# Column sums of shift and scale with 128 stationary columns in one product instead of four products of 32

## What is computed

```
c_act = silu(c)                                   # 1024 values
for i in range(2):
    shift, scale, gate = split(c_act @ mod_w[i] + mod_b[i], 3)     # mod_w[i]: 1024 x 3072
    h = rms_norm(x, norm_g[i]) * (1 + scale) + shift
    y = retention(h, ...) if i == 0 else forgetting_attention(h, ...)
    x = x + gate * y
```

## Time and profile before

| | |
|---|---|
| median of three runs | 694.55 us (694.49 to 694.74) |
| the profiled execution | 694.77 us, its span 693.0 us |
| PE busy | 679.8 us, 98% of the span |
| DVE, ACT busy | 502.2 us (72%), 380.4 us (55%) |
| products and loads of PE | 4590, 4591 records |
| bytes moved | 138.81 MB, 200 GB/s on average |

### The profile page before, as it was taken

The page is one execution under the profiler, slowest core; times in us unless marked ns, Lnnn a source line. Parts: engine busy times, 40 slices in busy tenths (PEclk is TensorE's granted clock), DMA queues, the critical chain, the costliest instruction groups (busy, mean ns, idle before and its releaser), DMA issues.

```text
span 693.0 us, 11560 instructions
## 1 busy us (share of the span) xinstructions
PE 679.8 (98%) x4590; PEld 554.2 (80%) x4591; DVE 502.2 (72%) x803; ACT 380.4 (55%) x561; POOL 16.3 (2%) x35
## 2 busy tenths in 40 slices
PE   8899999999999999999999999999999999999996
PEld 4679997777878888878788877778888888888885
DVE  6888988787986779766768889777665555565445
ACT  5457434565555665654655765845574444444444
POOL 4010000000000000000000000000000000000000
PEclk9999999999999999999999999999999999999999
DMA  9999785667896176833455654434656666655511
GB/s 295 368 377 391 272 265 174 201 223 230 303 339 213 51 245 225 274 128 106 135 157 158 190 164 137 139 122 120 212 156 212 182 190 178 197 185 189 186 61 61
DMA packets 74405, 138.81 MB, mean 200 GB/s; under 512 B 5732, under 2 KB 18400, under 8 KB 74352
## 3 DMA queue, kind: packets, MB, share of 16 engines
q1 hardware_dynamic: 72816, 134.92, 60.1%
q10 hardware_dynamic: 736, 1.81, 0.7%
q0 software_dynamic: 800, 1.35, 0.6%
HBM read 137.01 MB, written 1.05 MB: 199 GB/s over the span
## 4 chain that ended last, share of the span: by engine, by line
PE 90%; DVE 3%; SPq 2%; DMA 1%; ACT 1%; issue 1%; DVEq 0%; ACTq 0%
PE G L392 23%; PE G L394 22%; PE G L393 22%; PE T L433 5%; PE G L412 2%; PE G L413 2%; PE G L414 2%; PE T L791 2%; DMA arena<-in_mod_w_dram 1%; PE T L779 1%; DVE wlo L1119 1%; SPq L2547 1%; PE G L529 1%; PE G L531 1%; PE G L530 1%
## 5 line engine op out<-in xcount | busy, mean ns | idle before, releaser
L1119 DVE TENSOR_TENSOR wlo<-raw,whi 128x1024 fp32r<-128x1024 f32 x202 | 245.6, 1222 | 111.3 <-ACT whi L1927 110.9
L1927 ACT ACTIVATE whi<-raw 128x1024 fp32r<-128x1024 f32 x202 | 211.9, 1060 | 133.4 <-PE G L394 89.5
L392 PE MATMUL G<-whi,ahi 128*128 128x512 f32 x694 | 280.4, 404 | 0.2 <-DVE wlo L1119 0.2
L394 PE MATMUL G<-whi,alo 128*128 128x512 f32 x694 | 271.1, 391 | 0.0
L393 PE MATMUL G<-wlo,ahi 128*128 128x512 f32 x694 | 270.4, 390 | 0.0
L392 PEld LDWEIGHTS G<-whi,ahi 128*128 128x128 f32 x694 | 130.3, 188 | 29.3 <-issue 1.8
L394 PEld LDWEIGHTS G<-whi,alo 128*128 128x128 f32 x694 | 130.3, 188 | 28.4
L393 PEld LDWEIGHTS G<-wlo,ahi 128*128 128x128 f32 x694 | 130.6, 188 | 25.3 <-issue 1.0
L1929 ACT ACTIVATE arena<-T,st 128x128 f32<-128x128 f32 (+2 forms) x56 | 21.8, 476 | 30.0 <-DVE st L1520 30.0
L1927 ACT ACTIVATE ahi<-T 128x512 fp32r<-128x512 f32 x25 | 14.9, 597 | 39.6 <-PE T L433 39.6
L1929 ACT ACT_TABLE_LOAD x27 | 34.6, 1283 | 3.3 <-issue 1.8
(11 more groups left out here) (254 smaller groups left out, 628.8 us busy)
## 6 DMA issues: line engine op xcount, KB each, us to landing
raw<-in_ret_w_in_dram SPq DMA_DIRECT2D x48, 512.0 KB, 6.2
raw<-in_w_gate_up_dram SPq DMA_DIRECT2D x40, 512.0 KB, 4.0
raw<-in_mod_w_dram SPq DMA_DIRECT2D x32, 512.0 KB, 4.7
raw<-in_fox_w_in_dram SPq DMA_DIRECT2D x32, 512.0 KB, 4.6
raw<-in_w_in_dram SPq DMA_DIRECT2D x28, 512.0 KB, 3.7
raw<-in_w_down_dram SPq DMA_DIRECT2D x22, 512.0 KB, 3.5
arena<-in_mod_w_dram SPq DMA_DIRECT2D x16, 512.0 KB, 9.6
raw<-in_ret_w_out_dram SPq DMA_DIRECT2D x16, 512.0 KB, 5.1
```

The costliest lines, as they stand in the source:

```text
L392: e.matmul(o, ah, wh, start=first and k == 0, stop=False)
L394: done = e.matmul(o, al, wh, start=False, stop=last and k == 1)
L1119: e.tensor_tensor(o, a, b, op).then_inc(sig[name], 1)
L1927: d = e.activation(o, a, f, scale=scale)
```

## The change

The diff has four parts. In `own_rows` and `other_rows` the loop over four ranges of 32 columns goes, and one product has 128 stationary columns. POOL waits for the fifth count of `macc` (DVE's sum of the last group) instead of the 12th of `mod0`. The forget gates' high and low parts lie in turns of 16 columns (`narrow`), so that one product of 32 stationary columns gives both the high-by-high and the low-by-high part, in 32 partitions; high by low stays a product of 16. `zT` has 32 rows, and `turn_forget` replaces the transposes by products with a constant matrix that adds row r and row r + 16 while it turns them.

```
-        zT = PTf[0:16, 0, 0:S]
+        zT = PTf[0:32, 0, 0:S]
+        narrow = ahi[:, 29, :].rearrange("p (k t n) -> p k t n", t=2, n=16)
...
                 for r in range(r0, 8):
-                    for c in range(0, P, 32):
-                        e.matmul(o[c:c + 32, :], mod_tile(g)[:, a, r, i * P + c:i * P + c + 32], cact[:, r:r + 1].to_broadcast([P, 32]), start=r == r0, stop=False)
+                    e.matmul(o, mod_tile(g)[:, a, r, i * P:i * P + P], cact[:, r:r + 1].to_broadcast([P, 32]), start=r == r0, stop=False)
...
-                for c in range(0, P, 32):
-                    d = e.matmul(sums_at(SUMMED[g][i], a)[c:c + 32, :], macc[:, g % 2, a, i * P + c:i * P + c + 32], ones[:, 0:32], start=False, stop=True)
-                return d
+                return e.matmul(sums_at(SUMMED[g][i], a), macc[:, g % 2, a, i * P:i * P + P], ones[:, 0:32], start=False, stop=True)
...
             def turn_forget():
                 on_.wait_ge(sig["forget"], 1)
+                on_.wait_ge(sig["head2_in"], 32)
                 t = bank("forget_t", sig["forget"], 2)
                 for m in range(2):
-                    d = e.transpose(t[:, 16 * m:16 * m + 16], zT[:, m * P:(m + 1) * P], idf[0:16, 0:16])
+                    d = e.matmul(t[:, 16 * m:16 * m + 16], zT[:, m * P:(m + 1) * P], head[0:32, C_SEL:C_SEL + 16], start=True, stop=True)
...
-                e.matmul(t[0:16, 0:S], wh, ahi[:, k, :], start=k == 0, stop=False)
-                e.matmul(t[0:16, 0:S], wl, ahi[:, k, :], start=False, stop=False)
-                d = e.matmul(t[0:16, 0:S], wh, alo[:, k, :], start=False, stop=k == 7)
+                e.matmul(t[0:32, 0:S], ahi[:, 29, 32 * k:32 * k + 32], ahi[:, k, :], start=k == 0, stop=False)
+                d = e.matmul(t[0:16, 0:S], narrow[:, k, 0, :], alo[:, k, :], start=False, stop=k == 7)
...
-                    tt(ahi[:, 29, P:2 * P], raw_tile(n), ahi[:, 29, 0:P].bitcast(F32), ALU.subtract, "used")
+                    tt(narrow[:, :, 1, :], raw_tile(n).rearrange("p (k n) -> p k n", n=16), narrow[:, :, 0, :].bitcast(F32), ALU.subtract, "used")
...
-                    copy(zT, T[bank_of["forget"]][0:16, 0:S], "forget")
+                    copy(zT, T[bank_of["forget"]][0:32, 0:S], "forget")
...
-                        act(ahi[:, 29, 0:P], raw_tile(n), ACT.Copy, "narrow_hi")
+                        act(narrow[:, :, 0, :], raw_tile(n).rearrange("p (k n) -> p k n", n=16), ACT.Copy, "narrow_hi")
...
-            on_.wait_ge(sig["mod0"], 12)
+            on_.wait_ge(sig["macc"], 5)
             e.dma_start(posi, pos_in.partition_broadcast(P).rearrange("p a n -> p (a n)")).then_inc(sig["small_in"], 16)
```

More of the change, by code:

```diff
@@ L725, in _ @@
             t = bank("forget", sig["forget"], 1)
-            nhi, nlo = ahi[:, 29, 0:P], ahi[:, 29, P:2 * P]
             for k in range(8):
@@ L729, in _ @@
                 on_.wait_ge(*ready[k, 1])
-                wh, wl = nhi[:, k * 16:(k + 1) * 16], nlo[:, k * 16:(k + 1) * 16]
-                e.matmul(t[0:16, 0:S], wh, ahi[:, k, :], start=k == 0, stop=False)
-                e.matmul(t[0:16, 0:S], wl, ahi[:, k, :], start=False, stop=False)
-                d = e.matmul(t[0:16, 0:S], wh, alo[:, k, :], start=False, stop=k == 7)
+                e.matmul(t[0:32, 0:S], ahi[:, 29, 32 * k:32 * k + 32], ahi[:, k, :], start=k == 0, stop=False)
+                d = e.matmul(t[0:16, 0:S], narrow[:, k, 0, :], alo[:, k, :], start=False, stop=k == 7)
             d.then_inc(sig["forget_pe"], 1)
```

## The result

The changed kernel takes 700.69 us (699.74 to 702.30), the kernel before 694.74 us in the same comparison: the ratio is 1.0088, with a 95% interval of 1.0076 to 1.0100. One of the five executions of the kernel before took 977.55 us, the others 694.49 to 694.88; the ratio leaves it out. The change makes the kernel slower, and by more than the 0.2% that can be told from none. The forecast was 699.4, 1.3 us too little, with a range of 697.7 to 701.0. The profiled execution is the quickest of the five: 699.74 us, its span 697.9 us, 4.9 us longer than before. Its mean granted clock is 0.999. The other executions, 700.4 to 702.3 us, have 0.991 to 0.997; what stands behind that comes with the experiments.

The account below looks back on a forecast made before the run. PE, busy 98% of the span, was taken as the bound, with the sums on the path in each stage. Stages +5.55 and forget gates -0.7 us on 694.55 gave 699.4 us, range 697.7 to 701.0.

Parts of the forecast that it names:

- The price of a 128-column record: PE's sums: each record of 128 stationary fp32 columns takes 110 ns, against 42 ns for four of 32.
- The rival of 42 ns: PE's sums: a 128-column record costs only 42 ns, giving a faster kernel, 693.6 us; chance 0.05.
- The stages: Groups 0 to 4 before the last `rows_unit`: longer sums delay it by 2.65 + 1.4 + 1.5 = +5.55 us.
- PE's wait for `macc`: In front of PE's sums: the wait gets shorter in group 2 and is gone in group 0.
- Forget gates: PE's forget products: 8 of 24 go, -0.91 us, turning costs +0.2; net -0.7 us.
- The moved transfers: DVE's first sum into `acc`: rows of `mod_b` land up to 6.3 us later; cost taken as 0.
- the bound of 1: Upper limit of +1 us for DVE standing at its first sum into `acc` for the moved transfers.
- The sum: Whole kernel: +5.55 - 0.7 = +4.85 us, giving 699.4 us.
- the clock: Behind the sums: PE's clock falls to 1.2 GHz, 2.7 us more once or twice, 702 to 705 us; chance 0.04.
- the late rows of `mod_b`: DVE stands 1 us or more for these rows, and PE with it: 700.4 us; chance 0.06.

Follow-up runs that it names:

- experiment 5: Kernel before with the sums as two products of 64 stationary columns instead of four of 32: 695.87 us, ratio 1.0021.
- experiment 6: Changed kernel with 2 moving columns instead of 32 in the 128-column sums: 703.65 us, ratio 1.0123.
- experiment 3: Kernel before with only POOL's small transfers moved, waiting for `macc` 5 instead of `mod0` 12: 695.90 us, ratio 1.0017.
- experiment 4: Changed kernel with the 32-column sums back, joined forget products and moved transfers kept: 695.61 us, ratio 1.0012.
- experiment 1: Kernel before with only the 128-column sums in `own_rows` and `other_rows`: 702.18 us, ratio 1.0108.
- experiment 10: Changed kernel with POOL's small transfers waiting for `mod0` 12 again: 700.67 us, ratio 1.0086.
- experiment 7: Kernel before with 128-column products in `own_rows` only, `other_rows` keeping its four of 32: 703.21 us, ratio 1.0117.
- experiment 9: Changed kernel with bf16 filler products where PE waits, before the first sums and in group 2: 699.86 us, ratio 1.0075.
- experiment 2: Kernel before with only the joined forget products: 694.07 us, ratio 0.9993.
- experiment 11: Kernel before with joined forget products and, in groups 2 to 4, all own records before the first of DVE's sums: 693.71 us, ratio 0.9987.
- experiment 8: Kernel before with joined forget products and four blocks instead of six for DVE in group 2: 700.32 us median, one execution 694.27.
- experiment 12: Kernel before with 64-column sums and four blocks instead of six for DVE in group 2: 695.90 us, ratio 1.0015.

## Why the prediction was right, and where it fell short

**The price of a 128-column record.** Forecast 110 ns, measured 108 in the changed kernel and 111 with two moving columns. Experiments 5 and 6 show that it is the stationary width of one range. The rival of 42 ns, and with it a faster kernel by wider sums, is out.

**The stages.** Group 2's sums end at 29.87 (29.48 + 0.39), forecast 29.85; `macc` is there at 27.45, forecast 27.5, and ACT's `x0_high` at 19.70, forecast 19.65. The first `rows_unit` behind it is 2.67 us late, forecast 2.65. Group 3 adds 1.24 (forecast 1.4) and group 4 1.47 (forecast 1.5), and the last `rows_unit` starts at 56.10, 5.4 us late, forecast 5.55. That PE's wait for `macc` would get shorter in group 2 was wrong: 0.96 us against 1.02, since DVE and PE moved alike. In group 0 it is gone, as forecast.

**Forget gates.** Net 0.6 of forecast 0.7 us: 16 products of 0.114 us in place of 24 as forecast, the turning 0.1 us dearer than thought.

**The moved transfers.** The place was right, DVE's first sum into `acc`, and so was the cost that I took, none, but only for the changed kernel, and there by luck: DVE comes there at 59.14 instead of 54.22 and finds the rows landed, 1.8 to 2.0 us after their issue and not up to 6.3. My reason for the 0 was another one, that PE uses the low parts behind that sum only 3 to 5 us later; in experiments 3 and 4, where DVE does stand, PE waits for such a low part (0.4 and 0.9 us). Taken alone the edit costs 1.2 us and in experiment 4 about 1.5, above the bound of 1 that I had given, since DVE stood 2.3 and 3.5 us. I had priced the edit behind the delay that another part of the change makes.

**The sum, and the term that it lacks.** 4.85 us were forecast and 4.97 measured between the two profiled executions. The medians are 6 us apart. What I left out of the sum, with a chance of 0.04, is the clock. It falls to 1.2 GHz in or behind 128-column sums: those of groups 0 and 2 in the profiled executions of experiments 1 and 10, group 3 too in experiment 7, all five in experiment 6. The mean clocks, 0.995 or less in every execution of experiments 1, 6 and 7 and 0.991 to 0.997 in four of the changed kernel, say that it fell there too; no trace shows where in those four. The kernel of experiment 10 takes 701.6 to 702.3 us with a mean clock of 0.990 to 0.993 and 699.1 to 699.7 with 0.999; over the changed kernel's five executions and these six, seven lie below 0.998. At half the clock the falls could cost half the time that they last. They cost less, for PE had waits to give: about 10 us at 0.50 make experiment 10's last `rows_unit` 2.6 us later than the changed kernel's (58.66 against 56.10), about 7 us make experiment 1's 1.2 us later. I had read that PE with 3.08 us busy of 4.40 keeps 1.00 and took it to hold for the new sums; but those records had four ranges side by side. The rival had the right mechanism, a price of 2.7 us for each fall where 1 to 3 us came for two, and a chance that was far too small. The range reached up to 701.0 for the late rows of `mod_b`, not for the clock; that it holds the median of 700.69 is in part luck, and one of the five executions, 702.30, lies above it.

What stays open: why the falls come in one execution and not in the next. A wait of PE in front of group 0's sums may have a part in it. In the profiled executions with 128-column sums PE stood 0.79 to 1.33 us there where the clock fell for group 0 (experiments 1, 6, 7 and 10), and 0.60 or not at all where it didn't (the changed kernel, experiment 9). The wait alone isn't enough: with 32-column sums PE stood 1.00 to 1.39 us in experiments 2, 3, 4 and 11, and nothing fell. For group 2 the wait doesn't tell the executions apart, 0.96 us without a fall (the changed kernel) and 0.97 and 0.95 with one (experiments 1 and 10). No run changed the wait and nothing else.

Open is also the cause of the 5.1 us of experiment 8: it goes when the number of PE's instructions in the sums is halved (experiment 12), which fits an engine that ran out of instructions while the DMA queues were full (a share of 1.08 between 26 and 31 us), but a late load of instructions was not itself seen: the one packet on the profile's queue for instructions between 20 and 33 us passes between 28 and 29, in experiment 2, which has no gap, as in experiment 8.

## What to carry to other kernels

Count the time between starts, not the instructions: four products of 32 stationary columns that go to four ranges of output partitions cost 42 ns where one of 128 costs 110, and joining them loses where few columns move (2 or 32 here). Joining pays where the moving columns set the pace, as in the forget products, 0.113 us each with 256 moving columns, whether 16 or 32 are stationary. And one execution's profile doesn't show what the others pay: set its clock beside theirs before taking its time for the kernel's. A transfer that is moved later must be priced with and without the delays that the other parts of the change bring.

## What the runs showed of the hardware that was not expected

Wide loads with few moving columns can cost twice. In experiment 6 records with 2 moving columns took as long as with 32, and PE's clock went to 0.50 for all five groups (703.65 us); with 32 moving columns it did so for two groups in experiments 1 and 10, three in experiment 7, one in experiment 9 and none in the changed kernel's profiled execution. With the four ranges of 32 or the two of 64 it fell in no profiled execution, but for the one that stood 5 us first (experiment 8).

A change between 128 and 32 stationary columns takes near 0.12 us, the mean of the two directions (experiment 7). The Trainium skill (TensorEngine Tiling (Array Packing), Key Properties) says that changing the tiling mode drains TensorE; a time that is lost at each change agrees with it.

The same two rows of `mod_b` took 4.3 to 5.0 us to land in experiment 3 and 1.8 to 2.0 us in the changed kernel, where they were issued 2.2 us later. The stretch of 50 to 55 us of experiment 3, and then two of the changed kernel; the column before the last is the DMA share:

```profile
50.00:55.00 5.00, 4.51 (x20) 3.40 (x20) 3.87 (x6) 3.64 (x6) 2.49 (x5) 1.00 1.06 376
```

```profile
50.00:55.00 5.00, 5.00 (x37) 4.59 (x36) 2.43 (x7) 1.40 (x3) 2.88 (x6) 1.00 0.82 275
55.00:60.00 5.00, 4.46 (x20) 3.39 (x19) 4.59 (x7) 3.26 (x5) 0.70 (x2) 1.00 0.54 140
```

The changed kernel's rows were issued at 53.42 and 53.94 and had landed by 55.9; between 53 and 56 us the share is 0.41 there. In experiment 3 they were under way from 51.2 to 56.7, with a share of 1.01 between 51 and 57 us. So the same 8 and 4 KB took more than twice as long beside full queues.
